# Order of the 512-column and 256-column products in the FFN up/gate and output projections of a two-block fp32 kernel

## What is computed

```python
# first block
x = x + jnp.einsum('bsd,de->bse', merged, w_out[l])
h = rmsnorm(x, norm2_g[l])
up = causal_dwconv(jnp.einsum('bsd,df->bsf', h, w_up[l]), ffn_conv_w[l], ffn_conv_b[l])
act = jax.nn.gelu(up) * jnp.einsum('bsd,df->bsf', h, w_gate[l])
x = x + jnp.einsum('bsf,fd->bsd', act, w_down[l])
...
# second block
x = x + y @ w_out[l]
h = rmsnorm_2(x, ffn_norm_g[l])
x = x + (jax.nn.silu(h @ w_gate[l]) * (h @ w_up[l])) @ w_down[l]
```

## Time and profile before

| | |
|---|---|
| median of 3 runs | 793.52 us (793.29 to 793.99) |
| profiled execution, first to last instruction (span) | 791.6 us |
| between span and median of the runs | 1.9 us |
| TensorE matmuls busy | 785.2 us, 4248 of them |
| weight loads busy | 672.4 us, 4248 of them |
| VectorE / ScalarE busy | 588.9 / 455.3 us |
| L1621 (512 columns) | 832 matmuls |
| L1623 (256 columns) | 832 matmuls |

### The profile page before, as it was taken

How to read it: one execution, slowest core, us unless ns; L and a number is a source line. 1 busy time by engine, 2 the same in 40 slices (tenths; PEclk the granted TensorE clock), 3 DMA queues, 4 the chain that set the end, 5 groups by cost and what they waited for, 6 DMA issues and landing times.

```text
span 791.6 us, 11285 instructions
## 1 busy us (share of the span) xinstructions
PE 785.2 (99%) x4248; PEld 672.4 (85%) x4248; DVE 588.9 (74%) x728; ACT 455.3 (58%) x597; POOL 48.6 (6%) x77
## 2 busy tenths in 40 slices
PE   9999999999999999999999999999999999999997
PEld 9998888888888888888888897888788888888886
DVE  6986897656578998878887877766788666666664
ACT  7679765676345654454545758767455545354444
POOL 0220331000000000000000041400000000000000
PEclk9999999999999999999999999999999999999999
DMA  8645545443446454554544552444445545454521
GB/s 329 241 174 195 197 181 213 154 160 138 181 160 213 156 209 167 206 202 175 204 167 159 185 198 90 153 164 156 140 147 221 206 166 199 172 205 169 208 106 53
DMA packets 21860, 140.85 MB, mean 178 GB/s; under 512 B 3394, under 2 KB 3522, under 8 KB 5826
## 3 DMA queue, kind: packets, MB, share of 16 engines
q1 hardware_dynamic: 21682, 140.13, 49.1%
q10 hardware_dynamic: 144, 0.26, 0.1%
HBM read 139.33 MB, written 1.05 MB: 177 GB/s over the span
## 4 chain that ended last, share of the span: by engine, by line
PE 99%; DVE 1%; ACT 0%; issue 0%
PE pp L1621 24%; PE pp L1582 18%; PE pp L1586 18%; PE pp L1585 18%; PE pp L1623 12%; PE pp L1740 1%; PE pp L1766 1%; PE pp L1753 1%; PE pp L1729 1%; PE pp L1910 1%; PE pp L1895 1%; PE pp L1902 0%; PE pp L1899 0%; PE pp L1803 0%; PE pp L1675 0%; PE pp L1687 0%
## 5 line engine op out<-in xcount | busy, mean ns | idle before, releaser
L980 DVE TENSOR_TENSOR wlo<-raw,whi 128x2048 fp32r<-128x2048 f32 x129 | 296.4, 2299 | 83.9 <-ACT whi L541 83.4
L541 ACT ACTIVATE whi<-raw 128x2048 fp32r<-128x2048 f32 x129 | 246.6, 1912 | 96.5 <-PE pp L1586 81.0
L1621 PE MATMUL pp<-ahilo,whi 128*128 128x512 f32 x832 | 261.9, 396 | 0.1
L1623 PEld LDWEIGHTS pp<-ahilo,wlo 128*128 128x128 f32 x832 | 156.3, 188 | 36.7
L1623 PE MATMUL pp<-ahilo,wlo 128*128 128x256 f32 x832 | 163.5, 278 | 0.0
L1582 PE MATMUL pp<-whi,ahilo 128*128 128x512 f32 (+1 forms) x336 | 133.9, 398 | 0.0
L1586 PE MATMUL pp<-whi,ahilo 128*128 128x512 f32 (+1 forms) x336 | 130.5, 388 | 0.0
L1585 PE MATMUL pp<-wlo,ahilo 128*128 128x512 f32 (+1 forms) x336 | 130.3, 388 | 0.0
L1621 PEld LDWEIGHTS pp<-ahilo,whi 128*128 128x128 f32 x832 | 128.3, 189 | 2.0 <-DVE wlo L980 0.3
L797 ACT ACTIVATE qk<-pp 128x512 f32<-128x512 f32 x44 | 26.3, 599 | 118.5 <-PE pp L1623 118.3
L1582 PE MATMUL pp<-whi,ahi 128*128 128x512 f32 (+1 forms) x228 | 89.2, 391 | 0.0
(11 more groups left out here) (247 smaller groups left out, 814.2 us busy)
## 6 DMA issues: line engine op xcount, KB each, us to landing
raw<-in_slabs SPq DMA_DIRECT2D x125, 1024.0 KB, 4.8
raw<-in_slabs SPq DMA_DIRECT2D x2, 832.0 KB, 4.4
first<-in_first SPq DMA_DIRECT2D x2, 768.0 KB, 7.8
first<-in_first SPq DMA_DIRECT2D x3, 384.0 KB, 4.6
raw<-in_slabs SPq DMA_DIRECT2D x2, 576.0 KB, 3.7
raw<-in_slabs SPq DMA_DIRECT2D x2, 512.0 KB, 10.1
out<-gg SPq DMA_DIRECT2D x3, 256.0 KB, 2.1
xa<-in_final_norm_g SPq DMA_DIRECT2D x1, 512.0 KB, 6.3
```

The source lines that it names most:

```text
L541: e.activation(whi[slot][:, :], raw[slot][:, :], ACT.Copy).then_inc(hi_ready, 1)
L980: e.tensor_tensor(wlo[slot][:, :], raw[slot][:, :], whi[slot][:, :].bitcast(f32), ALU.subtract).then_inc(lo_ready, 1)
L1621: e.matmul(out[:, m, :], w[m][0], act[:, k, :], start=k == 0, stop=False, skip_group_check=True)
L1623: ins = e.matmul(out[:, m, 0:SEQ], w[m][1], act[:, k, 0:SEQ], start=False, stop=k == KD - 1, skip_group_check=True)
```

## The change

In each chunk, the 512-column and then the 256-column product of weight tile 0 are issued, then those of tile 1: H0 L0 H1 L1 in place of H0 H1 L0 L1. The number and the shapes of the instructions, the operands, the waits and the instruction that raises `group_done` (L1 of the last chunk) are the same.

```diff
                 for k in range(KD):
                     ready(k)
-                    w = [weights(slot, k, slice(P * m, P * m + P), WIDE) for m in range(2)]
                     for m in range(2):
-                        e.matmul(out[:, m, :], w[m][0], act[:, k, :], start=k == 0, stop=False, skip_group_check=True)
-                    for m in range(2):
-                        ins = e.matmul(out[:, m, 0:SEQ], w[m][1], act[:, k, 0:SEQ], start=False, stop=k == KD - 1,
+                        hi, lo = weights(slot, k, slice(P * m, P * m + P), WIDE)
+                        e.matmul(out[:, m, :], hi, act[:, k, :], start=k == 0, stop=False, skip_group_check=True)
+                        ins = e.matmul(out[:, m, 0:SEQ], lo, act[:, k, 0:SEQ], start=False, stop=k == KD - 1,
                                        skip_group_check=True)
                 return ins
```

## The result

The changed kernel takes 797.46 us (median of 5 runs, 796.97 to 797.63) against 793.51 us before (793.29 to 793.99): ratio 1.0047, 95% interval 1.0037 to 1.0058. It is 3.95 us slower, and the spans of the two profiled executions differ by the same: 795.6 against 791.6 us.

A forecast was written before the change was run, and what follows sets the result against it. TensorE's matmul spacing was taken as the bound (99% of the chain); all terms were zero except two more size changes per chunk, +3 ns x 416 = +1.3 us, so 793.5 + 1.3 = 794.8 us, range 792.0 to 798.0.

The forecast's parts named there:

- slow rival: L0 to H1 and L1 to H0': a load under a lone L is late; up to +5.7 us, 799.2, halfway 796.4; chance 0.20.
- the prediction's own sign: Profile after: a down slab or strip changing its time, or TensorE waits over 1 us, would make the reasoning wrong.
- The bound and the multiplier: TensorE's matmul spacing sets the time; 416 chunks, so one ns per chunk is 0.42 us.
- The terms put at zero: Added or removed instructions, DMA, moved waits, and adding twice in a row into the same columns: each zero.
- two more changes of size per chunk, +3 ns, +1.3 us: Within each chunk, four switches between 512 and 256 columns instead of two, 1.5 ns each, over 416 chunks.
- A down slab still at 5.45 us: Expected in the profile after: the down slab behind up and gate slabs keeps its time of 5.45 us.
- fast rival: In each chunk, H costs its long-run distance and a lone L stays short: 683 ns, 788.0 to 789.5 us; chance 0.11.
- the pair L0 L1 is what costs: Two short products in a row delay H0'; separating them removes 3 ns per chunk, -1.3 us, 792.2; chance 0.10.
- side note on the load: A 128-column weight load, estimated at 107 ns, has next to no slack under an L in either order.

The follow-up runs named there:

- banks_0110: Order H0 H1 L1 L0 against the kernel before, so two of four neighbours write the same bank; 793.45 us in one run, 793.38 for the kernel before.
- two_chunks: Against the kernel before, 512-column products of two chunks are issued first, then their 256-column ones; 795.73 us in one run, 2.35 more.
- hlhl_384: The kernel after with 384 instead of 256 columns in the second product of each tile; 842.61 us in one run.
- hhll_384: The kernel before with 384 instead of 256 columns in the second products; 846.70 us in one run.
- after_gap: The kernel after with one more wait: gate slabs of FFN loop steps wait until ScalarE has copied the up slab's banks; 822.64 us in one run.

## Why the prediction was right, and where it wasn't

- **The range held** (792.0 to 798.0), but the outcome, slower by more than 0.2%, had been given only 0.25 where no measurable difference had 0.62. That 797.46 lies inside is in part luck: the range was drawn to take in most of the slow rival, whose mechanism the runs don't bear out.
- **By the prediction's own sign the reasoning was wrong.** It said that a down slab with another time would make it so whatever the total, and the down slab went from 5.45 to 5.50 us. The up and gate slabs took 11.29 us, not 11.19.
- **The bound and the multiplier held.** TensorE's spacing was all that moved, 99% of the chain, with no new wait. 288 of the 416 chunks are in the 18 slow steps, and there a chunk with its share of the down slab costs 12.9 ns more (207 / 16).
- **The terms put at zero held**: no wait, no DMA, the same clock, and adding into the bank just written (banks_0110 equals the kernel before).
- **The term that failed is "two more changes of size per chunk, +3 ns, +1.3 us".** It measured +10 ns per chunk in the slow slabs (353.3 x 2 against 696.6) plus 53 ns per down slab, 4.0 us in all, three times the forecast. The direction was right. The step of reasoning behind it, that the excess of a mixed stream is a price per change that can be carried to another order, was wrong: per change it measured 1.7 ns for H H L L, 10 ns in two_chunks (153 ns over 16 changes in a step), 4.1 ns for H L H L in the slow rhythm with its exit (260 over 64), zero in the fast one, 10 ns between long runs (20 for a pair, one change each way).
- **"A down slab still at 5.45 us" failed**: what a slab leaves behind is paid in the next one, 5.50 us. I had seen 0.01 us of this in the earlier trace rows and had not asked how it grows with another order.
- **The slow rival had the nearest size and the wrong mechanism.** Half of its upper end was 796.4, its end 799.2; measured 797.5. Its rows, H at 235 and L at 120 ns, are near what H and L read in the slow rhythm (233 to 241, and 113 to 120). But the load it blamed is not the cause, by hlhl_384 and by the fast slabs.
- **The fast rival's 683 ns per chunk is in no trace.** The fast slabs of the kernel after go at 693.3 ns, the level that the small rival, *the pair L0 L1 is what costs*, gave to every chunk; but only 80 of the 416 chunks do, and the same order at 353.3 ns per half chunk speaks against its mechanism.
- One sum of the fast rival doesn't come out: with the first chunk's 0.68 us for each, the gain would be 7 us, not 4 to 5.5. The start records have 686 ns for that chunk, which gives 4.3. And in its side note on the load the prediction says that the trace has no row for it; the earlier trace rows records one, at 188 ns.
- The formula of the Trainium skill, "TensorE: Matmul & The Clock Gate" (Back-to-back issue gap), knows only a matmul's own columns, so by it the two orders cost the same. The page calls it the isolated gap and says that in a stream of loads and matmuls both set the spacing, without a word on order. The measured difference, 10 ns per chunk in the slow slabs, decides against the formula for streams of mixed widths.

What stays open is what in the hardware makes the rhythm. The runs show that it depends on the sequence of widths and on how a slab was entered, not on banks, and that a longer product over each load doesn't remove it; the periodic sums sit 3.3, 13.3, 13.1 and 26.6 ns per chunk over those of long runs (before, after in its slow rhythm, hlhl_384, hhll_384). Which entries lead to the fast rhythm was not found: an added gap and another neighbour at the gate slab didn't.

## What to carry to other kernels

When TensorE is the bound, read the distance from start to start over a whole slab and the one behind it; the recorded durations overlap and hardly show such losses (their means went from 396 and 278 to 398 and 280 ns here). In long runs of one width a matmul cost the same here from first to last; a mixture of two widths cost 0 to 27 ns per four matmuls more, depending on the pattern, and its price couldn't be carried from one pattern to another. Group equal widths where nothing waits between chunks, keep the chunk's order where a wait stands in each, and measure.

## What the runs showed of the hardware that was not expected

- One instruction sequence has two steady paces in the same execution, 346.7 and 353.3 ns for a pair of 512 and 256 columns, and kept the fast one for 31 chunks in a row (second block) and the slow one for 37 (first block).
- A stream of 512-column matmuls needed five distances (27 ns in excess) to settle behind a long run of 256-column ones, at a granted clock of full level throughout.
- At the lower clock, granted after 3.68 us without a matmul, the pair took 640 ns, its columns and nothing more (after_gap).
- A gap of 1.11 us turned a slab that was fast without it into a slow one (after_gap, second block).
- Going from 256 to 384 columns in the short product turned the ranking of the two orders round: from 4.0 us in favour of H H L L to 4.1 us in favour of H L H L.
